# A hybrid decoder step: token norms of x by one-column matmuls, and a new order of the first loads and products

## The reference, cut to what matters

```python
mod = silu(c) @ w_ada + b_ada                 # 1024 -> 3 * 1024
shift, scale, gate = split(mod, 3)
h = rms_norm(x, g_norm) * (1 + scale) + shift
proj = h @ w_in                               # 1024 -> 7 * 1024
y_a = conv_branch(...)                        # GLU, depthwise conv of 31 taps, LayerNorm, silu, w_a_out
y_b = pool_branch(...)                        # causal means over 2, 4, 8, 16 tokens, w_grp, w_b_out
m = sigmoid(merge_a) * y_a + sigmoid(merge_b) * y_b
x = x + gate * (m @ w_out)
y = rms_norm(x, g_final)
```

## Time and profile before

| | us |
|---|---|
| three runs, median (lowest to highest) | 995.64 (995.27 to 995.8) |
| the profiled execution, whole time | 995.86 |
| its span | 993.7 |
| TensorE busy in the span | 971.8 |
| VectorE busy | 694.6 |
| ScalarE busy | 252.7 |

### The profile page before, as it was taken

How to read it: one execution, slowest core, us unless ns; L and a number is a source line. 1 busy time by engine, 2 the same in 40 slices (tenths; PEclk the granted TensorE clock), 3 DMA queues, 4 the chain that set the end, 5 groups by cost and what they waited for, 6 DMA issues and landing times.

```text
span 993.7 us, 14662 instructions
## 1 busy us (share of the span) xinstructions
PE 971.8 (98%) x6196; PEld 958.9 (97%) x6196; DVE 694.6 (70%) x687; ACT 252.7 (25%) x264; POOL 1.9 (0%) x12
## 2 busy tenths in 40 slices
PE   4999999999999999999999999999999999999997
PEld 3799999999999999999999999999999998999996
DVE  6878988627898772889864689978788743342346
ACT  5531112221122221111222111122633512122242
POOL 0000000000000000000000000000000000000000
PEclk9999999999999999999999999999999999999998
DMA  9611221231131231222024112213871173125104
GB/s 376 246 43 56 95 81 54 85 122 44 64 111 34 86 117 58 64 86 97 27 75 143 43 66 100 65 54 123 320 283 63 30 310 128 44 87 190 43 1 170
DMA packets 31960, 106.39 MB, mean 107 GB/s; under 512 B 7712, under 2 KB 14112, under 8 KB 28448
## 3 DMA queue, kind: packets, MB, share of 16 engines
q1 hardware_dynamic: 28304, 92.82, 26.8%
q10 hardware_dynamic: 3600, 12.72, 3.3%
HBM read 82.74 MB, written 22.79 MB: 106 GB/s over the span
## 4 chain that ended last, share of the span: by engine, by line
PE 96%; DVE 1%; DMA 1%; ACT 1%; SPq 0%; issue 0%; DVEq 0%
PE ps L463 31%; PE ps L466 31%; PE ps L464 31%; DMA bf<-x_t 1%; PE aux L415 1%; DVE stage_hi L886 1%; PE aux L449 0%; PE aux L421 0%; DVE hf L1159 0%; ACT hf L710 0%; PE aux L635 0%; PE aux L627 0%; ACT w_hi L678 0%; ACT L716 0%; SPq L302 0%; DVE bf L900 0%
## 5 line engine op out<-in xcount | busy, mean ns | idle before, releaser
L464 PE MATMUL ps<-hr,w_hi 128*128 128x344 f32 x1536 | 486.7, 320 | 0.0
L463 PE MATMUL ps<-hr,w_hi 128*128 128x344 f32 x1344 | 426.4, 320 | 0.0
L928 DVE SCALAR_TENSOR_TENSOR conv_y<-conv_u,par,conv_y 128x1024 f32<-128x1024 f32 x240 | 308.0, 1283 | 20.6 <-PE ps L466 14.1
L464 PEld LDWEIGHTS ps<-hr,w_hi 128*128 128x128 f32 x1536 | 288.9, 188 | 0.0
L466 PE MATMUL ps<-hr,w_lo 128*128 128x344 f32 x1344 | 285.0, 320 | 0.0
L463 PEld LDWEIGHTS ps<-hr,w_hi 128*128 128x128 f32 x1344 | 252.7, 188 | 1.7 <-issue 1.7
L466 PEld LDWEIGHTS ps<-hr,w_lo 128*128 128x128 f32 x1344 | 224.7, 188 | 0.0
L678 ACT ACTIVATE w_hi<-w_raw 128x1024 fp32r<-128x1024 f32 (+1 forms) x88 | 87.5, 996 | 270.8 <-PE ps L466 270.8
L862 DVE TENSOR_TENSOR w_lo<-w_raw,w_hi 128x1024 fp32r<-128x1024 f32 (+1 forms) x88 | 101.2, 1150 | 52.0 <-ACT w_hi L678 46.7
L463 PE MATMUL ps<-gr,w_hi 128*128 128x344 f32 x384 | 123.3, 323 | 0.0
L464 PE MATMUL ps<-gr,w_hi 128*128 128x344 f32 x384 | 121.8, 320 | 0.0
(11 more groups left out here) (128 smaller groups left out, 590.8 us busy)
## 6 DMA issues: line engine op xcount, KB each, us to landing
w_raw<-w_main SPq DMA_DIRECT2D x80, 512.0 KB, 3.6
ada_raw<-w_ada SPq DMA_DIRECT2D x8, 1024.0 KB, 16.9
bf<-x_t SPq DMA_DIRECT2D x4, 1032.0 KB, 8.6
sig_a<-stage_lo ACTq DMA_DIRECT2D x8, 516.0 KB, 2.7
sig_b<-stage_hi ACTq DMA_DIRECT2D x8, 516.0 KB, 2.6
y_conv<-conv_y SPq DMA_DIRECT2D x8, 516.0 KB, 2.9
silu_z<-stage_hi ACTq DMA_DIRECT2D x8, 516.0 KB, 4.2
bf<-y_conv SPq DMA_DIRECT2D x4, 1032.0 KB, 6.9
```

What stands on the lines that cost most here:

```text
L463: nc.tensor.matmul(out, wh, rhs_hi[:, cols(c)], start=(k == 0), stop=False)
L464: nc.tensor.matmul(out, wh, rhs_lo[:, cols(c)], start=False, stop=False)
L928: return v.scalar_tensor_tensor(out=y, in0=conv_u[:, x, k:k + SEQ], scalar=par[:, x, k:k + 1], in1=y, op0=ALU.mult, op1=ALU.add)
```

## The change

What it does:

- The sums of squares are made by TensorE alone, tile by tile: for each block of 128 tokens the squares are the stationary operand and one column of ones moves (`square_sums`). That leaves sums with tokens on the partitions, 128x8 for the prompt and 8x1 for the samples.
- Root and reciprocal are taken on these 128x8 and 8x1. `spread_rstd` multiplies each column, repeated over 128 columns, with a unit matrix, which puts the row on all partitions in PSUM; ScalarE and VectorE copy it to `row_rstd`.
- `h_hi` writes the high part straight from the scaled tile with the shift as bias, in one operation; `h_lo` adds the shift and subtracts the high part in one operation. The samples get operations of their own for both parts.
- Of the weights of jobs 0 and 1 only the first halves are loaded ahead of modulation block 0, the second halves behind it; they are split in halves too. The small tables are loaded from ScalarE's queue.
- The order of TensorE and the numbers of filler matmuls are changed.

The diff, cut to its core ("..." marks what is left out):

```diff
-WARM_ADA = ((0, 4), (0, 8), (0, 0), (0, 0))
-WARM_TURN = (3, 9, 0, 0)
-WARM_FIRST = 4
+WARM_SPREAD = 8
+WARM_ADA = 8
+WARM_TURN = 6
+WARM_FIRST = 20
...
 def _(sp):
...
             for s in range(2):
-                sp.dma_start(w_raw[:, s, :], t["w_main"][s]).then_inc(raw_full[s], 16)
+                sp.dma_start(w_raw[:, s, 0:HALF], t["w_main"][s][:, 0:HALF]).then_inc(first_half_loaded[s], 16)
             for q in range(4):
-                if q == 1:
-                    sp.dma_start(pick[:], t["pick"]).then_inc(small_loaded, 16)
...
                 for half in range(2):
...
+                if q == 0:
+                    for s in range(2):
+                        sp.dma_start(w_raw[:, s, HALF:], t["w_main"][s][:, HALF:]).then_inc(raw_full[s], 16)
...
 def _(pe):
...
+            def square_sums(e):
+
+                for b in range(XBS):
+                    last = nc.tensor.matmul(x_sums[:, b:b + 1], hf[:, e, b * P:(b + 1) * P], ones[:, 0:1],
+                                            start=(e == 0 and b == 0), stop=(e == KT - 1 and b == XBS - 1))
+                    if b == 0:
+                        nc.tensor.matmul(x_sums[0:NSAMP, XBS:XBS + 1], hf[:, e, SEQ:TOK], ones[:, 0:1], start=False, stop=False)
+                return last
+
+            def spread_rstd():
+
+                pe.wait_ge(x_inverse_ready, 1)
+                for b in range(XBS):
+                    last = nc.tensor.matmul(ps[:, 0, b // 4, b % 4 * P:(b % 4 + 1) * P], x_rstd[:, b:b + 1].broadcast_to([P, P]),
+                                            eye[:], start=True, stop=True)
+                    if b % 4 == 3:
+                        last.then_inc(x_spread, 1)
+                pe.wait_ge(x_inverse_ready, 2)
+                nc.tensor.matmul(ps[:, 0, 2, 0:NSAMP], x_rstd[0:NSAMP, XBS:XBS + 1].broadcast_to([NSAMP, P]),
+                                 eye[0:NSAMP, 0:NSAMP], start=True, stop=True).then_inc(x_spread, 1)
...
-            pe.wait_ge(x_squared, KT - 2)
-            keep_warm(WARM_SUMS)
-            pe.wait_ge(x_summed, 1)
-            token_sums(aux[:, 0, 0:CW], sq_sum[:, cols(0)], x_var_done)
-            token_sums(aux[:, 1, 0:CW], sq_sum[:, cols(1)], x_var_done)
-            token_sums(ps[:, 1, 1, 0:CW], sq_sum[:, cols(2)], x_var_done)
+            for e in range(KT):
+                pe.wait_ge(x_squared, e + 1)
+                if e == 0:
+                    keep_warm(WARM_SUMS)
+                last = square_sums(e)
+            last.then_inc(x_var_done, 1)
+            keep_warm(WARM_SPREAD)
+            pe.wait_ge(small_loaded, 64)
+            spread_rstd()
...
+            keep_warm(WARM_ADA)
+            ada(0)
+            keep_warm(WARM_TURN)
+            turn(0)
+            keep_warm(WARM_FIRST)
+            ada(1)
+            first_steps(0)
+            turn(1)
+            first_steps(1)
+            ada(2)
+            first_steps(2, [0])
+            turn(2)
+            first_steps(2, [1])
+            ada(3)
+            first_steps(3, [0])
+            turn(3)
+            first_steps(3, [1])
+            for k in range(4, together):
+                first_steps(k)
...
 def _(act):
...
+            act.dma_start(pick[:], t["pick"]).then_inc(small_loaded, 16)
...
             def h_hi(e):
...
-                nc.scalar.activation(bf[:, e, 0:SEQ], bf[:, e, 0:SEQ], ACT.Identity, bias=mod[:, e // 2, e % 2, 0:1]).then_inc(h_shifted, 1)
-                act.wait_ge(h_shifted, e + 1)
-                nc.scalar.activation(hr[:, e, :], bf[:, e, :], ACT.Copy).then_inc(h_hi_done, 1)
+                nc.scalar.activation(hr[:, e, 0:SEQ], bf[:, e, 0:SEQ], ACT.Identity, bias=mod[:, q, j, 0:1]).then_inc(h_hi_done, 1)
...
-            for s in range(2):
-                split_hi(s, KT * P, 16)
-            for c in range(CHUNKS):
...
+            act.wait_ge(x_var_done, 1)
+            nc.scalar.activation(x_rstd[:, 0:XBS], x_sums[:, 0:XBS], ACT.Sqrt, bias=eps[:, 0:1]).then_inc(x_std_ready, 1)
...
 def _(dve):
...
-            for e in range(1, KT):
-                dve.wait_ge(x_squared, e + 1)
-                link(v.tensor_tensor(sq_sum, hf[:, 0, :] if e == 1 else sq_sum, hf[:, e, :], ALU.add))
...
-            for c in range(CHUNKS):
-                dve.wait_ge(x_std_ready, c + 1)
-                link(v.reciprocal(row_rstd[:, cols(c)], row_rstd[:, cols(c)]))
+            dve.wait_ge(x_std_ready, 1)
+            v.reciprocal(x_rstd[:, 0:XBS], x_rstd[:, 0:XBS]).then_inc(x_inverse_ready, 1)
...
             for q in range(4):
                 modulation(q)
+                h_tile(2 * q)
                 h_samples(q)
-                h_tile(2 * q)
                 if q >= 1:
                     h_lo(2 * q - 1)
                 h_tile(2 * q + 1)
-                if q == 0:
-                    split_lo(1, KT * P, 2)
                 h_lo(2 * q)
+                if q == 1:
+                    first_split(0, 1)
+                    first_split(1, 1)
```

More of the change, by code:

```diff
@@ L47 @@
 QUADS = P // QUAD
+XBS = SEQ // P
 TOKBS = 4
@@ L175, in build @@
         pick = g_place("pick", [NMOD], F32)
-        eye = g_place("eye", [TOKB], F32)
+        eye = g_place("eye", [P], F32)
         tok_rstd = g_place("tok_rstd", [CHUNKS * TOKBS], F32)
+        x_rstd = g_place("x_rstd", [XBS + 1], F32)
         mod = g_place("mod", [6, ADA_BLOCKS, NMOD], F32)
@@ L427, in keep_warm, with ada @@
                 for _ in range(n):
-                    nc.tensor.matmul(ps[:, 0, 0, 0:P], ones[:], ones[:], start=True, stop=True)
-            def ada(q, half):
-                if (q, half) == (0, 0):
+                    nc.tensor.matmul(ps[:, 1, 1, 0:P], ones[:], ones[:], start=True, stop=True)
+            def ada(q):
+                if q == 0:
                     pe.wait_ge(c_ready, 1)
[L433 to L440, removed]
+                if q == 2:
+                    pe.wait_ge(x_std_ready, 2)
+                if q == 3:
+                    pe.wait_ge(ada_mod_done, 2)
+                for half in range(2):
+                    pe.wait_ge(ada_loaded[q][half], 16)
+                    for k in range(half * KT // 2, (half + 1) * KT // 2):
+                        last = modulation_product(ada_bank[q], k, ada_raw[:, q, :, :])
+                last.then_inc(ada_done, 1)
@@ L494, in _, with first_steps @@
             together = KT - 3
-            def side_by_side(k):
+            def first_steps(k, jobs=(0, 1)):
                 if k == 0:
                     pe.wait_ge(w_lo_done, 2)
-                    pe.wait_ge(ada_mod_done, 2)
-                    pe.wait_ge(x_std_ready, CHUNKS)
+                if k == KT // 2:
+                    pe.wait_ge(w_lo_done, 4)
                 pe.wait_ge(h_lo_done, k + 1)
[L502 to L507, removed]
-                if q == 0:
[L509 to L522, removed]
+                for i in jobs:
+                    h_step(i, k)
+            keep_warm(WARM_ADA)
[17 more added lines that the diff above has]
+                first_steps(k)
             for i in range(2):
@@ L635, in spread @@
                     last = nc.tensor.matmul(aux[:, c % 2, b * TOKB:(b + 1) * TOKB], column.broadcast_to([TOKB, P]),
-                                            eye[0:TOKB, :], start=True, stop=True)
+                                            eye[0:TOKB, 0:TOKB], start=True, stop=True)
                 last.then_inc(f_spread, 1)
@@ L680, in _ @@
             act.dma_start(c_in[:], t["c_t"]).then_inc(c_loaded, 16)
+            act.dma_start(pick[:], t["pick"]).then_inc(small_loaded, 16)
+            act.dma_start(ada_b[:], t["ada_b"]).then_inc(small_loaded, 16)
+            act.dma_start(vecs[:], t["vecs"]).then_inc(small_loaded, 16)
+            act.dma_start(eye[:], t["eye"]).then_inc(small_loaded, 16)
             act.sem_inc(act_evac, 2)
@@ L701, in h_hi, with first_split @@
             def h_hi(e):
+                q, j = e // 2, e % 2
                 act.wait_ge(h_scaled, e + 1)
-                nc.scalar.activation(bf[:, e, 0:SEQ], bf[:, e, 0:SEQ], ACT.Identity, bias=mod[:, e // 2, e % 2, 0:1]).then_inc(h_shifted, 1)
-                act.wait_ge(h_shifted, e + 1)
-                nc.scalar.activation(hr[:, e, :], bf[:, e, :], ACT.Copy).then_inc(h_hi_done, 1)
+                nc.scalar.activation(hr[:, e, 0:SEQ], bf[:, e, 0:SEQ], ACT.Identity, bias=mod[:, q, j, 0:1]).then_inc(h_hi_done, 1)
+                if j == 0:
+                    act.wait_ge(h_samples_ready, q + 1)
+                    nc.scalar.activation(hr[:, e:e + 2, SEQ:TOK], bf[:, e:e + 2, SEQ:TOK], ACT.Copy).then_inc(h_samples_hi, 1)
+            def first_split(s, half):
+                n = slice(half * KT * P // 2, (half + 1) * KT * P // 2)
+                act.wait_ge((raw_full if half else first_half_loaded)[s], 16)
+                nc.scalar.activation(w_hi[:, s, n], w_raw[:, s, n], ACT.Copy).then_inc(w_hi_done, 1)
             for e in range(KT):
@@ L881, in modulation, with first_split @@
```

(28 more changed lines are left out.)

48 lines of the change are left out of this document (27 added, 21 removed).

## The result

| | before | after |
|---|---|---|
| median of the runs (lowest to highest), us | 995.54 (995.27 to 995.8) | 1026.79 (1026.6 to 1027.66) |
| span of the profiled execution, us | 993.7 | 1025.9 |
| first real product, us | 33.60 | 57.43 |
| first product of job 2, us | 62.26 | 94.48 |

The changed kernel is slower by 3.2%: ratio 1.0316, 95% interval 1.0298 to 1.0334. The spans of the two profiled executions differ by 32.2 us, and the start of job 2 moved by 32.2 us (94.48 - 62.26). So all of the loss lies ahead of job 2, and nothing of it was taken up or added later. (The profiled execution of the changed kernel is the longest of its four, 1027.66 us; by the medians the loss is 31.25 us.)

The account below looks back on a forecast made before the run. TensorE, busy without a gap from 47.98 us on, was taken as the bound, so the start decides. Its serial terms put job 2 at 90.3 instead of 62.26: 995.86 + 28.0 - 0.2, some 1023.5 us, range 1009 to 1030.

Parts of the forecast that it names:

- the likeliest case: TensorE's clock falls during the one-column sums of squares: 1018 to 1030 us, chance 0.61.
- The clock: In the sums: falls to half rate under one-column matmuls, 27.3 us if low throughout, 14.7 if never low.
- the first rival: In the sums: the clock stays high since weight loads count as work; +15.1 us, so 1011; chance 0.30.
- The pitch: In the sums: the load of 128 weight columns sets each matmul's time, 0.2235 us; 14.7 us in all at high clock.
- the small matmul: In each tile's sums: the matmul with 8 weight columns, taken at 0.05 us.
- High spell: Early in the sums: clock high from about 12.4 to 15.7 us, saving 3.4 us.
- From the sums to the first product: Fillers, spread, modulation products and turn on TensorE: 16.1 us, plus 2.2 for coming from the low clock.
- The third turn and the wait behind it: Behind the first product: turn(1) adds 0.9 us, idle TensorE until h_lo(1) 3.8, a possible clock drop 1.5.
- Terms of nothing: Load order and splitting, separate samples, shorter h_hi pass, loop and tail: claimed to cost nothing more.

Follow-up runs that it names:

- e5: The changed kernel with 128 equal columns of ones moving in each matmul of the sums instead of one, into two banks; 1014.75 us.
- e2: The changed kernel with turn(1) ahead of first_steps(0) instead of behind it; 1024.44 us.
- e6: The changed kernel with the whole weights of jobs 0 and 1 loaded ahead of modulation block 0 again; 1026.76 us.
- e11: The changed kernel with both 128 moving columns in the sums and turn(1) ahead of first_steps(0); 1010.07 us.
- e12: e11 with the four filler constants behind the sums (WARM_SPREAD, WARM_ADA, WARM_TURN, WARM_FIRST) set to 0; 1006.31 us.
- e4: The changed kernel with the eight tiles of squares added on VectorE first, then one set of nine one-column matmuls; 1009.88 us.
- e1: The changed kernel with 56 equal columns of ones moving in the sums of squares instead of one; 1023.56 us.

## Why the prediction was right

It said 1023.5 us in 1009 to 1030, with the clock falling as the likeliest case; it is 1026.8. The sum against the profile, term by term:

| | predicted | measured |
|---|---|---|
| start of the sums | 12.05 | 11.96 |
| end of the sums | 36.0 | 38.1 |
| from there to the first product | 18.3 | 19.3 |
| from there to job 2 | 36.0 | 37.05 |
| delay of job 2 | 28.0 | 32.2 |

- *The clock*. The step that chose between 1011 and 1023 was the one from the tail's rows to the new stage, and it held. Those rows alone could not carry it: PE had waited 0.8 us in that stretch and had ended its work at 987.0, before the clock fell at about 987.4. The 0.30 for the first rival said as much; it took e5 to show the cause. The Trainium skill (TensorE: Matmul & The Clock Gate, "Why this matters for your kernels") warns of idle gaps between bursts; the trace agrees at the second fall, behind 3.65 us of idle PE at 61 to 65 us, but at the first one the clock fell with PE busy throughout, which that section doesn't cover. The first rival's price, +15.1 us, was some 4 us short: e5, which is that case, measured +19. Its job 2 starts at 80.98 instead of 77.4: 1.8 us of that lie in the sums, 0.4 ahead of the first product, and 1.3 behind it, where the clock fell at the wait.
- *The pitch*. Taken at 0.2235 us a matmul at the high clock and 0.42 at the low, with 0.05 for each small matmul of the samples. Inside a group of eight the pitch is as forecast: narrow windows of e5's timeline show its records 0.11 us apart, two to a matmul (12.37 to 13.04 for six steps), the changed kernel's as well (13.14 to 14.37 for eleven), and 0.214 apart at the low clock (20.86 to 22.14 for six). The term that was mis-sized is the small matmul. With the changes between 128 and 8 weight columns around it, it adds 0.32 us to each tile at the high clock (2.11 less 8 times 0.2235), and some 0.2 at the low one. Sums wholly at the low clock took 28.9 us in e2, not 27.3.
- *High spell*. One was expected, from 12.4 to 15.7 us, to save 3.4 us; there was one, until about 16.4, and against e2's sums it saved 2.9. This term and the small matmuls are the 2.1 us by which the sums ended late. That there was one at all was not certain, as e2 shows.
- *From the sums to the first product*. E5 ran this stage wholly at the high clock and took 16.6 us (28.58 to 45.14), where the sum has 16.1; the low clock at its head cost 2.7 us, not 2.2. That makes the 1.0 us. That PE's own fillers set the end, not VectorE, was right: h_lo of tile 0 was ready by 56.05 and PE came to it at 57.43.
- *The third turn and the wait behind it*. 3.8 us of idle PE expected, 3.65 measured, with the releaser named; 0.28 and 0.36 at h_lo(3) and h_lo(6) where 0.5 and 0.7 were expected. The fall of the clock behind it was taken at 1.5 us and cost 2.7: the two k-steps took 5.46 us to the next product (64.98 to 70.44), against 3.04 in e2 (64.46 to 67.50), and that product 0.25 more.
- *Terms of nothing*. The order of loads moved nothing (e6), and neither did the loop and the tail: the span grew by as much as the start of job 2. No run separates the shorter h_hi and the samples' own operations; they were not waited for beyond the waits above.

What the account looks like from the runs: of 31 us, the low clock in and behind the sums is 12 (e5), the order of turn(1) 4.7 (e2, e11), the fillers 3.8 (e12, or up to 6.1 by its trace), and 10.8 remain between e12 and the kernel before (1006.3 - 995.5). These are steps taken one after another, and in another order they would have other sizes: e4 alone, from the changed kernel, is 17. The seven tiles of sums that stand in for VectorE's adds are 14.8 us of PE by themselves at the high clock, more than that remainder; that the reciprocals that went pay a part back is likely, but no run separates it.

## What to carry to other kernels

A reduction given to TensorE as many weight loads with one moving column is priced by its loads, and may be run at half the clock: look for the granted clock of such a stretch and the pitch of its records, not for its busy share. Where the clock matters, try more moving columns than are needed; the 128 of e5 cost nothing, since the load set the pitch. And before moving work from an engine off the path to the one that the end hangs on, add up that engine's program in order: VectorE's seven adds were nearly free: they ran while x was still landing and were done 1.6 us behind the last square (e4).

## What the runs showed of the hardware that was not expected

- With the same 128-column float32 weight loads back to back, the clock fell with 1 and with 56 moving columns (at about 16.4 and 18.2 us) and held with 128 (the profiled executions of the changed kernel, e1 and e5). PE was busy throughout in all three.
- Going between weights of 128 and of 8 columns costs more than the matmul of 8 itself: each tile of eight large matmuls and a small one took 2.11 us at the high clock, where eight at their own pitch take 1.79 (e5). Eight fillers took 1.98 us ahead of ada(0), whose weights have 32 columns (32.56 to 34.54), and 1.78 ahead of the spread, whose weights have 128 (28.58 to 30.36). Why was not tried.
- The clock rose ahead of the sums in the changed kernel's profiled execution and not in e2's, though the first 20 us are the same instructions. The sums ended 2.9 us apart for it (38.1 and 41.0). It can't be told from the source, and what decides it was not found.
- The granted clock reads 1.00 ahead of its first change in a trace, also where the records show half pace: in the changed kernel the weight loads of the first ten fillers take 4.2 us (7.74 to 11.96) with 1.00 shown, and in e2 the whole of the sums does. There only the durations tell.
